# Cross attention computed by pairs of heads: first pair's scores inside the query units, output projection contracted pair by pair

## What is computed

```python
q = (xn @ wq).reshape(b, s, 4, 256)                 # s = 256 positions, 4 heads
k, v = jnp.split(rmsnorm(mem, norm_mem) @ wkv, 2, axis=-1)   # 256 memory rows, 4 heads of 256
sc = jnp.einsum("bshd,bmhd->bhsm", q, k) * 256 ** -0.5
p = jax.nn.softmax(sc, axis=-1)
o = jnp.einsum("bhsm,bmhd->bshd", p, v).reshape(b, s, d)
h = h + o @ wo
```

## Time and profile before

| | |
|---|---|
| time, median of 3 runs | 2591.6 us (2590.25 to 2593.38) |
| the profiled execution's own time | 2594.49 us |
| its span (first to last instruction) | 2592.7 us |
| PE busy in it | 2312.9 us, 89% |
| DVE busy | 1714.8 us, 66% |
| ACT busy | 1336.3 us, 52% |
| HBM traffic | 595 MB read, mean 230 GB/s |
| mean granted PE clock | 0.937 of full |

### The profile page before, as it was taken

One profiled execution on the slowest core, in us unless ns is written; L12 is line 12 of the kernel. 1 busy time (PEld: TensorE's weight loads), 2 busy tenths in 40 slices (PEclk: granted clock), 3 DMA queues, 4 the chain that ended last, 5 costly groups with the idle time before them and its releaser, 6 DMA issues.

```text
span 2592.7 us, 30279 instructions
## 1 busy us (share of the span) xinstructions
PE 2312.9 (89%) x11625; PEld 1937.2 (75%) x11625; DVE 1714.8 (66%) x1515; ACT 1336.3 (52%) x1163; POOL 26.3 (1%) x50
## 2 busy tenths in 40 slices
PE   6998999897788999999999999998775898599996
PEld 5757899865677888888888888886765767588885
DVE  3324454594437888888898989897435714488886
ACT  3023433415316777767777777775432223267774
POOL 2000000000000000000000000000000000000000
PEclk9999899898978999999999999999885999799998
DMA  7242455530237999999999999997330241399993
GB/s 259 98 170 92 133 182 195 179 106 33 98 122 249 367 337 371 329 366 336 364 339 342 363 339 363 339 359 260 128 116 32 82 142 37 118 343 335 333 328 130
DMA packets 269353, 597.13 MB, mean 230 GB/s; under 512 B 9008, under 2 KB 33792, under 8 KB 269280
## 3 DMA queue, kind: packets, MB, share of 16 engines
q1 hardware_dynamic: 264944, 582.01, 62.9%
q0 software_dynamic: 4336, 14.10, 1.6%
HBM read 595.02 MB, written 1.05 MB: 230 GB/s over the span
## 4 chain that ended last, share of the span: by engine, by line
PE 85%; DVE 7%; ACT 4%; issue 2%; DMA 1%; ACTq 0%; POOL 0%; DVEq 0%; SPq 0%
PE ps L638 22%; PE ps L640 21%; PE ps L639 21%; PE ps L578 5%; PE ps L573 3%; PE ps L824 2%; PE ps L857 1%; PE ps L625 1%; DVE w_low L1777 1%; PE ps L773 1%; DMA ring<-in_ev_w_in 1%; PE ps L800 1%; PE ps L684 1%; ACT w_high L1286 1%; DVE w_low L1429 1%
## 5 line engine op out<-in xcount | busy, mean ns | idle before, releaser
L1777 DVE TENSOR_TENSOR w_low<-ring,w_high 128x2048 fp32r<-128x2048 f32 x432 | 983.7, 2289 | 137.2 <-ACT w_high L1286 136.2
L1286 ACT ACTIVATE w_high<-ring 128x2048 fp32r<-128x2048 f32 x432 | 822.9, 1916 | 180.6 <-PE ps L640 180.3
L639 PE MATMUL ps<-w_high,parts 128*128 128x512 f32 (+1 forms) x2024 | 790.5, 391 | 0.0
L638 PE MATMUL ps<-w_high,parts 128*128 128x512 f32 x1816 | 721.2, 397 | 30.5 <-DVE w_low L1777 26.8
L640 PE MATMUL ps<-w_low,parts 128*128 128x512 f32 x1816 | 710.9, 391 | 0.0
L639 PEld LDWEIGHTS ps<-w_high,parts 128*128 128x128 f32 x2024 | 384.9, 190 | 75.3
L638 PEld LDWEIGHTS ps<-w_high,parts 128*128 128x128 f32 x1816 | 343.0, 189 | 107.6 <-issue 35.6
L640 PEld LDWEIGHTS ps<-w_low,parts 128*128 128x128 f32 x1816 | 342.7, 189 | 73.6
L1429 DVE TENSOR_TENSOR w_low<-ring,w_high 128x2048 fp32r<-128x2048 f32 (+2 forms) x93 | 206.5, 2243 | 137.3 <-ACT w_high L1104 136.6
L1104 ACT ACTIVATE w_high<-ring 128x2048 fp32r<-128x2048 f32 (+2 forms) x93 | 173.2, 1874 | 225.9 <-PE ps L640 183.6
L638 PE MATMUL ps<-XT_high,w_high 128*128 128x256 f32 x896 | 259.1, 289 | 12.5 <-DVE parts L1418 6.2
(11 more groups left out here) (336 smaller groups left out, 1956.2 us busy)
## 6 DMA issues: line engine op xcount, KB each, us to landing
ring<-in_od_moe_gu SPq DMA_DIRECT2D x224, 1024.0 KB, 7.3
ring<-in_od_moe_down SPq DMA_DIRECT2D x112, 1024.0 KB, 6.9
ring<-in_w SPq DMA_DIRECT2D x96, 1024.0 KB, 7.0
ring<-in_ev_ffn_gu SPq DMA_DIRECT2D x22, 1024.0 KB, 7.6
ring<-in_xa_wkv SPq DMA_DIRECT2D x8, 2048.0 KB, 8.0
ring<-in_od_pw_w SPq DMA_DIRECT2D x6, 2048.0 KB, 8.7
ring<-in_w_in SPq DMA_DIRECT2D x6, 2048.0 KB, 7.9
ring<-in_ev_ffn_down SPq DMA_DIRECT2D x11, 1024.0 KB, 5.0
```

The source lines that it names most:

```text
L638: mm(out_, xh, wh, start=start, stop=False)
L639: mm(out_, xl, wh, start=False, stop=False)
L1286: A(w_high[:, j % SPLITS, :], ring[:, j % NS, :], ACT.Copy).then_inc(moe_sem(k, "high"), 1)
L1777: V.tensor_tensor(w_low[:, j % SPLITS, :], ring[:, j % NS, :], w_high[:, j % SPLITS, :].bitcast(F32), SUB)\
```

## The change

The attention is worked on in pairs of heads, (0, 1) and (2, 3), called pair 0 and pair 1. The new order on PE:

1. turn x; q0; first half of q1
2. scores of pair 0 (banks 4, 5)
3. second half of q1
4. transposes of the probabilities of pair 0, into the pair of banks of q0; wait until q1 is copied out
5. scores of pair 1 (banks 6, 7)
6. attended values of heads 0, 1 (banks 4, 5)
7. o0 over heads 0, 1 for all positions
8. transposes of pair 1 (banks 4, 5)
9. o1 over heads 0, 1 for the first 128 positions
10. attended values of heads 2, 3 (banks 6, 7)
11. o1 over heads 0, 1 for the other positions; o0 over heads 2, 3; o1 over heads 2, 3

The list of halves becomes q0, q0, q1, q1, o0, o1, o0, o1. The panel of o0 is thus released one half later in the list than before. The softmax of a pair works on 128 x 512 tiles where it worked on 128 x 1024: twice as many maxima, divisions and copies of transposed probabilities, each half as large; the exponentials stay eight blocks of 256. Besides, the probability tile and the counts of the softmax semaphores of the other, small attentions are renumbered, with the same work.

```diff
-            if src in ("x", "attended"):
+            if src == "attended":
+                if c0 == 0:
+                    pieces_split += [(len(panels) + j, "features", half, n) for half in range(2) for j in range(2)]
+                split_at[u] = len(pieces_split) - (4 if c0 == 0 else 2)
+                parts_end[u] = len(pieces_split) - (1 if c0 == 0 else 0)
+                release = ("parts_split", parts_end[u])
+            elif src == "x":
                 split_at[u] = len(pieces_split)
                 pieces_split += [(len(panels), "columns" if columns else "features", half, n) for half in range(2)]
-                release = ("parts_split", split_at[u] + 2)
+                parts_end[u] = len(pieces_split)
+                release = ("parts_split", parts_end[u])
...
@@ tensor engine
+                def scores(p):
+                    for tc in range(2):
+                        for h in (2 * p, 2 * p + 1):
+                            for c in range(2):
+                                last = mm(ps[:, 4 + 2 * p + tc, h % 2 * T:h % 2 * T + T], QT[:, 2 * h + c, tc * P:(tc + 1) * P],
+                                          KT[:, 2 * h + c, :], start=(c == 0), stop=(c == 1))
+                        last.then_inc(S("pair_scores"), 1)
+                def turn_pair(p, bank):
+                    for tc in range(2):
+                        pe.wait_ge(S("pair_probs"), 4 * a + 2 * p + tc + 1)
...
+                def output(j, half, tcs):
+                    u = UNIT[f"{tag}o{j}"]
+                    q = split_at[UNIT[f"{tag}o0"]] + 2 * half + j
+                    pe.wait_ge(S("parts_split"), q + 1)
+                    wh, wl = half_tile(q, w_high), half_tile(q, w_low)
+                    for tc in tcs:
+                        for i in range(4):
+                            kc, t = 4 * half + i, slice(tc * P, (tc + 1) * P)
+                            if i % 2 == 0:
+                                pe.wait_ge(S("attended_low"), 4 * a + kc // 2 + 1)
+                            last = product(PAIRS[u % 2][:, tc, :], (XT_high[:, kc, t], XT_low[:, kc, t]),
+                                           (wh[:, i, :], wl[:, i, :]), start=(kc == 0), stop=(kc == KC - 1))
+                    if tcs[-1] == 1:
+                        last.then_inc(S("parts_read"), 1)
...
+                turn(src, ready, value)
+                project(f"{tag}q0", first=True)
+                project(f"{tag}q1", halves=(0,))
+                for name in ("k0", "k1", "v0", "v1", "q0"):
+                    evicted(tag + name)
+                scores(0)
+                project(f"{tag}q1", halves=(1,))
+                turn_pair(0, 2 * (UNIT[f"{tag}q0"] % 2))
+                evicted(f"{tag}q1")
+                scores(1)
+                attend(0)
+                output(0, 0, (0, 1))
+                turn_pair(1, 4)
+                output(1, 0, (0,))
+                attend(1)
+                output(1, 0, (1,))
+                output(0, 1, (0, 1))
+                output(1, 1, (0, 1))
@@ scalar engine, after take_columns of q0
+                highs(halves_to(f"{tag}q1", 1))
+                softmax_pair(0)
+                highs(halves_to(f"{tag}q1", 2))
+                pair_columns(0, 2 * (UNIT[f"{tag}q0"] % 2))
+                softmax_pair(1)
+                for h in (0, 1):
+                    attended_high(h)
                 highs(halves_to(f"{tag}q1", 3))
+                pair_columns(1, 4)
+                for h in (2, 3):
+                    attended_high(h)
+                highs(halves_to(f"{tag}q1", 4))
@@ vector engine, after columns_low
+                lows(halves_to(f"{tag}q1", 1))
+                bias_pair(0)
+                normalise_pair(0)
+                lows(halves_to(f"{tag}q1", 2))
                 take_columns(f"{tag}q1", QT[:, 4:8, :])
+                pair_columns(0, 2 * (UNIT[f"{tag}q0"] % 2))
+                bias_pair(1)
+                for h in (0, 1):
+                    attended_low(h)
+                normalise_pair(1)
                 lows(halves_to(f"{tag}q1", 3))
+                pair_columns(1, 4)
+                for h in (2, 3):
+                    attended_low(h)
+                lows(halves_to(f"{tag}q1", 4))
                 for j in range(2):
                     add_unit(f"{tag}o{j}", j, ALPHA if tag == "C" else None)
```

More of the change, by code:

```diff
@@ L260, in program @@
         IDENT, ONES = c_("ident"), c_("ones")
-        prob = {n: w_(8192 if n in (3, 4) else 0, 2, 4, T) for n in range(1, 6)}
+        prob = w_(8192, 2, 4, T)
+        PROB, PROBT, QT, KT, VM = w_(0, 2, 4, T), w_(2048, KC, T), w_(10240, KC, T), w_(6144, KC, T), w_(8192, HALVES, D)
         ssq, var, std, rstd = sm(2), sm(2), sm(2), sm(2)
@@ L556, in _, with project @@
             mm = nc.tensor.matmul
-            seen = {"act": 0, "vector": 0, "attended": 0}
-            def project(name, first=False):
+            seen = {"act": 0, "vector": 0}
+            def project(name, first=False, halves=(0, 1)):
                 u = UNIT[name]
@@ L566, in project @@
                 if u in split_at:
-                    return project_parts(u, columns, n, pair, src, first)
+                    return project_parts(u, columns, n, pair, first, halves)
                 wait_panel(pe, unit_panel[u])
@@ L580, in project, with project_parts @@
                 last.then_inc(S(f"unit_ready{u % 2}"), 1)
-            def project_parts(u, columns, n, pair, src, first):
+            def project_parts(u, columns, n, pair, first, halves):
                 def columns_part(kc):
                     if first and kc % 2 == 0:
[L586 to L591, removed]
+                        pe.wait_ge(S("columns_by_vector"), seen["vector"] - 4 + kc // 2 + 1)
+                for half in halves:
                     q = split_at[u] + half
@@ L664, in memory_projections, with attention, attend, evicted @@
                     project(f"{tag}v{j}")
[L666 to L671, removed]
+            def attention(tag, a, src, ready, value):
+                def scores(p):
[8 more added lines that the diff above has]
+                        pe.wait_ge(S("pair_probs"), 4 * a + 2 * p + tc + 1)
+                        for g in range(2):
+                            for mc in range(2):
+                                last = nc.tensor.transpose(ps[:, bank + g, mc * T + tc * P:mc * T + (tc + 1) * P],
+                                                           PROB[:, tc, 2 * p + g, mc * P:(mc + 1) * P], IDENT)
+                    last.then_inc(S("pair_turned"), 1)
+                def attend(p):
+                    pe.wait_ge(S("pairT_by_act"), 2 * a + p + 1)
+                    pe.wait_ge(S("pairT_by_vector"), 2 * a + p + 1)
+                    for f in range(4 * p, 4 * p + 4):
+                        for mc in range(2):
+                            last = mm(ps[:, 4 + f // 2, f % 2 * T:f % 2 * T + T], VM[:, mc, f * P:(f + 1) * P],
+                                      PROBT[:, f // 2 * 2 + mc, :], start=(mc == 0), stop=(mc == 1))
+                        if f % 2:
+                            last.then_inc(S("attended"), 1)
+                def output(j, half, tcs):
[12 more added lines that the diff above has]
+                        last.then_inc(S("parts_read"), 1)
+                def evicted(name):
@@ L1906, in _ @@
                 for tc in range(2):
-                    last = normalise(4 + which, dst, tc)
+                    last = normalise(2 + which, dst, tc)
                 step(last)
```

112 lines of the change are left out of this document (64 added, 48 removed).

## The result

| | us | runs | ratio to before, 95% interval |
|---|---|---|---|
| before | 2591.57 (2590.25 to 2593.38) | 4 | 1 |
| the change | 2556.09 (2555.80 to 2559.53) | 4 | 0.9868 [0.9856, 0.9880] |
| predicted | 2558.0 (2554.0 to 2570.0) | | 0.987 |

A forecast was written before the change was run, and what follows sets the result against it. PE's work, stops and lowered clock in the attentions were taken as the bound; 10.6 - 0.3 + 12.6 + 10.7 = 33.6 us less, from the median 2591.6 to 2558.0, range 2554 to 2570.

The forecast's parts named there:

- The bound: PE is 85% of the chain; in A it stands 10.02 us in three stops, and transposes run at the lower clock.
- B's 1.9: First part of L684 in B at clock 0.50, 9.05 us instead of 7.14; saving 1.9, perhaps absent in the median run.
- The sum: End of q1 to end of attended values: 10.6, 12.6 and 10.7 us less in A, B, C; minus 0.3, 33.6 less.
- Step 1: Pair 0's scores before q1's second half: softmax lies behind q1 with 2.6 us to spare; transposes start unstopped at full clock.
- Step 2: Copy of q1 behind o1's low part on DVE: PE stands 0.95 us, 0.5 of it from the low part.
- Steps 3 and 4: Pair 1's scores, pair 0's values, then o0 over heads 0, 1: PE stands only 0.27 us, awaiting head 1.
- Step 5: From pair 1's transposes through o1's end: copies and splits are covered by output work, so PE has no stop.
- A's two low parts: Two next-layer low parts on DVE between A's two additions to H delay the addition of o1: 0.3 us given back.
- Queues: Rival: DVE's fixed order makes PE wait a whole 2.28 us low part at two places per attention: 2571.7 us; chance 0.14.
- Slow transposes: Rival: 16 transposes still take 3.61 us, 5.1 comes back: 2563.1 us; counted inside the forecast's own range, chance 0.76.
- The clock in the broken-up order: Rival: stops of 0.95 and 0.27 drop PE's clock, work behind takes twice its time, up to 2660 us; chance 0.04.
- No change: Rival: a shared buffer holds the whole chain as before, only the transposes move: 2590 us; chance 0.03.

The follow-up runs named there:

- the filled kernel: Kernel before, with 3, 15 and 3 float32 matmuls, results unused, in the three stops of each attention: 2586.2 us, ratio 0.9975.
- the pairwise output alone: Against the change: both halves of q1 come before the scores of both pairs, the rest by pairs as in the change: 2556.1 us.
- the second profile: The changed kernel itself, unaltered, executed and profiled again beside the kernel before: 2555.8 us, ratio 0.9866.
- the kernel with the long stop filled: Kernel before, with 13 more float32 matmuls, results unused, behind the scores in PE's stop before the transposes: 2589.5 us, ratio 0.9989.
- the hoisting alone: Against the change: pair 0's scores stay inside q1, but o0 and o1 begin only when both pairs are attended: 2568.9 us, again 2571.4.

## Why the prediction was right

**The bound.** That PE's stops and its clock in the old order were what could be taken held. The stops fell from 10.0 to 0.7 in each attention, 28.0 us in three. The 16 transposes held PE for 3.61; now the first eight take 1.03 and the other eight 0.79 (from 221.61 to the first product of o1 at 222.40), 5.4 less in three. With B's 1.9 that makes 35.3, all that the profile shows. The clock's share is 7.3 here, more than the 5.5 that the filled kernel gives, in part because there the second eight transposes still wait 0.26 for DVE. The sum had 10.02 less 1.22 of stops, three times (26.4), 5.1 for transposes at full clock, 1.9 for B's slow start, 0.45 for handovers, less 0.3.

**Step 1** held: DVE's division of pair 0 was over in the profile after, in A,

```profile
203.72 0.69 DVE L1595 TENSOR_TENSOR work<-work,small 128x512 f32<-128x512 f32 x1
205.32 2.29 DVE L1501 TENSOR_TENSOR w_low<-ring,w_high 128x2048 fp32r<-128x2048 f32 x1 [0.91 <-ACT w_high L1153]
207.53 1.22 DVE L1513 COPY work<-ps 128x1024 f32<-128x1024 f32 x1
...
216.65 0.69 DVE L1605 TENSOR_TENSOR parts<-ps,XT_high 128x512 fp32r<-128x512 f32 x1 [0.92 <-ACT XT_high L1210]
...
218.25 0.69 DVE L1595 TENSOR_TENSOR work<-work,small 128x512 f32<-128x512 f32 x1
```

at 204.4, which is 12.2 after the end of q0 (192.2; forecast 12.5), and PE went from q1 into the transposes without a stop. But what the step says hides the long stop is more than is needed, as the pairwise output alone shows. This the prediction didn't weigh: it costed the parts together and never one without the other.

**Step 2** was mis-sized: the stop was forecast at 0.95 and is 0.68. The low part of o1 ran 205.32 to 207.6, so the copy of q1 began at 207.53, only 0.3 behind the end of q1's products; 0.5 had been put down for it. PE's transposes are also 0.1 longer than the 0.96 assumed.

**Steps 3 and 4.** The stop of 0.27 inside o0, for head 1, isn't listed as a wait: its low part starts at 216.65, in the rows above, and is over at 217.34, when the first six products are. What is left of it is in the spacing of the products, 0.28 and 0.34 around the seventh where others are 0.23 apart, 0.16 in all.

**Step 5** held: in the profile nothing waits from there to the end. DVE's division of pair 1 starts for the last time at 218.25 and is over at 218.9, with PE in o0 until 221.6.

**A's two low parts** gave back 0.1, 0.3 forecast: the addition of o1 in A starts 0.14 after its last product (242.45), in B 0.03 after. That A is 0.25 longer than B in this profile (71.39, 71.14) is for the rest not theirs; in the second profile the two differ by 0.02.

**The sum** of the attentions was 10.3 + 12.6 + 10.7 = 33.6 against 35.3 measured, with most of the error in steps 2 and 4 (0.4 in each attention) and 0.2 in A's low parts. From its own terms it would have been 33.8; each attention was rounded down by a little. From the end of q0 to the end of o1 it took 50.2 us in A, 50.7 forecast. The gain wasn't given back in the layers behind: behind C the first profile after is 3.1 us longer than the one before, but the old order with its stops filled is 1.7 and 2.5 longer there too.

**B's 1.9.** I left it in the sum and called it luck. The one profile before has it in B; in the kernel with the long stop filled, 1.7 to 1.85 of slow values lie in A and C and none in B, and the kernel before, in 15 runs on one chip, lay between 2588.5 and 2593.8. How often its executions have this term isn't measured, so that the profile holds it is luck for the sum. The Trainium skill ("TensorE: Matmul & The Clock Gate", section "What's actually happening") says of a kernel's first matmuls that the number of slow ones changes from run to run; no run here looks at the first ones.

**The rivals.** Queues: no low part was paid beyond the 0.3 of step 2. Slow transposes: no. The clock in the broken-up order: 1.00 in all rows of the change; but the rival's mechanism is real, and nearer than I held it. In the hoisting alone, stops of 2.3 and 0.9 around eight transposes were enough to halve the clock for the work behind them, at 1.8 to 3.3 us an attention. The change has only a stop of 0.7, and with the pairwise output alone one of 0.92 leaves the clock at 1.00 too; how long a stop may be before it costs the clock wasn't measured. No change: no.

What isn't settled: how much of the 0.8 to 2.3 us that the hoisting takes off where the output doesn't hide pair 1 is its own. The 1.8 in C came twice; in the medians (2571.4 and 2572.5) it can't be told from chance.

## What to carry to other kernels

Where one engine works through a chain (scores, softmax, values) whose middle lies on other engines, cut the chain in two and lay the work that follows the first half, here its share of the output projection, beside the second half's middle; hoisting the start of the chain ahead of its own inputs' last unit added next to nothing once that was done. Price such a stop with what the lower clock takes behind it, here 7 us beside 28, and try each part of a change alone before crediting it. And compare two kernels by the stretch that the change touches, in the trace: two profiles of one kernel differed by 3.5 us before that stretch began.

## What the runs showed of the hardware that I had not expected

PE's clock fell from 1.00 to 0.50 around two stops of 2.3 and 0.9 us with eight transposes between them, in each of three attentions. The stop of 1.37 before the scores had not cost it in the kernel before. Filling the long stop of 7.25 alone only moved the slow stretch behind the transposes in A and C (8.99 and 8.83 us for values that take 7.14), and not in B. With fillers in all three stops the clock was 1.00 from 204 to 256 us in A, and the values took 7.14 in all three attentions.
